# Expert rows added to token sums in DRAM by an accumulating indirect DMA

## What is computed

```python
out = jnp.zeros_like(t)
for e in range(N_EXPERTS):                       # 16
    hid = jax.nn.silu(t @ w_gate[e]) * (t @ w_up[e])
    out = out + combine[:, e:e + 1] * (hid @ w_down[e])
...
x = x + _hmoe(_rmsnorm(x, g_ffn), ...)
y = _rmsnorm(x, g_final)
```

## Time and profile before

| | us |
|---|---|
| median of 3 runs | 1064.77 |
| lowest, highest | 1064.41, 1065.37 |
| the profiled execution's own time | 1067.34 |
| its span, first to last instruction | 1065.6 |
| PE busy | 970.6 (91%) |
| DVE, ACT, POOL busy | 656.9, 547.8, 279.2 |

### The profile page before, as it was taken

The page is one execution under the profiler, slowest core; times in us unless marked ns, Lnnn a source line. Parts: engine busy times, 40 slices in busy tenths (PEclk is TensorE's granted clock), DMA queues, the critical chain, the costliest instruction groups (busy, mean ns, idle before and its releaser), DMA issues.

```text
span 1065.6 us, 16632 instructions
## 1 busy us (share of the span) xinstructions
PE 970.6 (91%) x5991; PEld 856.6 (80%) x5991; DVE 656.9 (62%) x797; ACT 547.8 (51%) x609; POOL 279.2 (26%) x187
## 2 busy tenths in 40 slices
PE   3989899999999998999999999939899999999960
PEld 2989789978988996799999986827788888888750
DVE  5495649647774884611211112378999898989827
ACT  5644525624462553533333323356787878787622
POOL 2433304213140331443434353000311010101012
PEclk9999999999999999999999999969999999999985
DMA  9452122312221320132332359228999999999835
GB/s 305 134 166 60 46 58 73 85 39 69 79 64 39 89 59 20 49 91 79 90 88 79 99 177 303 83 106 284 408 413 414 413 414 413 414 413 414 313 125 202
DMA packets 146738, 193.67 MB, mean 182 GB/s; under 512 B 14486, under 2 KB 91692, under 8 KB 146576
## 3 DMA queue, kind: packets, MB, share of 16 engines
q1 hardware_dynamic: 139000, 165.27, 44.9%
q0 software_dynamic: 4656, 16.21, 4.0%
q10 hardware_dynamic: 3048, 11.75, 2.8%
HBM read 173.43 MB, written 19.77 MB: 181 GB/s over the span
## 4 chain that ended last, share of the span: by engine, by line
PE 71%; DVE 14%; issue 7%; ACT 4%; DMA 2%; DVEq 1%; POOL 0%; POOLq 0%; ACTq 0%; SPq 0%
PE PJ L447 58%; DVE MEM L1640 2%; DVE MEM_R L1859 2%; PE NM L1272 2%; PE PJ L1221 1%; PE MS L1455 1%; PE MS L1254 1%; PE MS L1292 1%; PE NM L447 1%; PE MS L1267 1%; PE MS L1299 1%; PE NM L1403 1%; PE MS L1282 1%; DMA MEM<-in_x_prompt_dram 1%; DMA MEM<-expert_rows,MEM 1%
## 5 line engine op out<-in xcount | busy, mean ns | idle before, releaser
L447 PE MATMUL PJ<-MEM_R 128*128 128x272 f32 (+2 forms) x5016 | 805.1, 321 | 14.5 <-ACT MEM L857 6.0
L447 PEld LDWEIGHTS PJ<-MEM_R 128*128 128x128 f32 x5016 | 723.9, 191 | 77.8 <-issue 10.6
L661 POOL TENSOR_TENSOR MEM_R<-RAW,MEM_R 128x1024 fp32r<-128x1024 f32 x81 | 198.5, 2459 | 357.1 <-ACT MEM_R L798 357.1
L1859 DVE TENSOR_TENSOR MEM_R<-CHUNK,MEM_R 128x2048 fp32r<-128x2048 f32 x100 | 224.6, 2286 | 15.4 <-ACT MEM_R L1055 14.1
L1055 ACT CAST MEM_R<-CHUNK 128x2048 fp32r<-128x2048 f32 x100 | 189.3, 1912 | 14.1 <-PE PJ L447 7.8
L798 ACT CAST MEM_R<-RAW 128x1024 fp32r<-128x1024 f32 x81 | 84.5, 1051 | 125.3 <-DMA RAW<-in_w_pb_dram 35.6
L1799 DVE TENSOR_TENSOR MERGED<-PJ,MEM 128x544 f32<-128x544 f32 x16 | 11.6, 724 | 146.9 <-PE PJ L447 146.9
L747 POOL COPY MEM<-MEM 128x1 uint32 (+1 forms) x16 | 20.7, 1297 | 235.1 <-PE MS L1455 235.1
L1640 DVE SCALAR_TENSOR_TENSOR MEM<-MEM 128x548 f32<-128x548 f32 x72 | 60.9, 846 | 8.5 <-DVE MEM L1638 0.9
L1064 ACT CAST MEM_R<-MS 128x1024 fp32r<-128x1024 f32 x17 | 17.3, 1016 | 33.6 <-PE MS L1455 33.6
L862 ACT ACTIVATE MEM<-MEM 128x548 f32<-128x548 f32 x16 | 10.6, 664 | 43.9 <-DVE MEM L1640 43.7
(11 more groups left out here) (282 smaller groups left out, 916.9 us busy)
## 6 DMA issues: line engine op xcount, KB each, us to landing
CHUNK<-in_w_gate_dram SPq DMA_DIRECT2D x34, 1024.0 KB, 9.7
CHUNK<-in_w_up_dram SPq DMA_DIRECT2D x34, 1024.0 KB, 11.3
CHUNK<-in_w_down_dram SPq DMA_DIRECT2D x34, 1024.0 KB, 9.7
RAW<-in_w_in_dram SPq DMA_DIRECT2D x56, 512.0 KB, 3.7
expert_rows<-MEM ACTq DMA_DIRECT2D x16, 512.0 KB, 6.0
expert_rows<-MEM SPq DMA_DIRECT2D x8, 512.0 KB, 5.2
RAW<-in_w_pa_dram SPq DMA_DIRECT2D x8, 512.0 KB, 3.6
RAW<-in_w_pb_dram SPq DMA_DIRECT2D x8, 512.0 KB, 3.6
```

The costliest lines, as they stand in the source:

```text
L447: ins = pe.matmul(out, w(a), x(b), start=first and n == 0, stop=last and n == 2)
L661: tt(lo, raw[slot], hi.bitcast(F32), ALU.subtract).then_inc(lo_done, 1)
L1859: tt(moe_hl[c][1], moe_raw[c], moe_hl[c][0].bitcast(F32), ALU.subtract).then_inc(chunk_lo[c], 1)
```

## The change

Two DRAM tensors are new. `token_sums` has one row for each token; POOL stores the residual `x2` there before the second gather. `choice_weights` has one word for each pair of token and expert: DVE makes it (`choice`), POOL stores it. DVE also makes `choice_id`, which is 16 times the token plus the tile's expert, for each place.

Empty places now hold 544, one more than the last token. The gather, the gather of weights and the scatter have a bounds check that skips such places; the gather's tile is cleared once, so that skipped rows hold something.

After a tile's gather POOL waits until ACT has copied the result out, then adds it to `token_sums` with an accumulating indirect DMA, then gathers the next tile's 128 weights into one column. ACT multiplies by this column as it copies the result out. An accumulation is only started after the one before it has landed. The last tile waits in the same way, and then SP loads the sums in five plain loads; the ten gathers and DVE's `add_rows` are gone. So are `expert_rows`, its stores, and the zero tile. `choice_weights` stands before `stage(1)`, and two DVE instructions on slots are gone. POOL's wait for the second gather's tile and the two new stores stand before its `stage(1)`.

```diff
             for m in range(NE, TILES):
-                sp.dma_start(y_dram[m * P:(m + 1) * P, :], zeros).then_inc(rows_zeroed, 16)
...
+            await_step(sp, sums_out, last * 16 + 16 * (J + 1))
+            for j in range(J):
+                sp.dma_start(ya[0:rows_of[j], j, :], sums_dram[tok(j), :]).then_inc(ya_in[j], 16)
...
+            pool.memset(xg, 0.0).then_inc(xg_cleared, 1)
+            pool.wait_ge(xg_cleared, 1)
             def gather_rows(index):
-                pool.indirect_dma_start(out=xg, out_offset=None, in_=t_dram,
-                                        in_offset=bass.IndirectOffsetOnAxis(ap=index, axis=0)).then_inc(xg_in, 16)
+                pool.indirect_dma_start(out=xg, out_offset=None, in_=t_dram, in_offset=row(index),
+                                        bounds_check=N - 1, oob_is_err=False).then_inc(xg_in, 16)
+            def gather_weight(out, index, landed):
+                pool.indirect_dma_start(out=out, out_offset=None, in_=choice_dram, in_offset=row(index),
+                                        bounds_check=N * NE - 1, oob_is_err=False).then_inc(landed, 16)
+            def add_to_sums(index, rows):
+                pool.indirect_dma_start(out=sums_dram, out_offset=row(index), in_=rows, in_offset=None,
+                                        bounds_check=N - 1, oob_is_err=False, compute_op=ALU.add).then_inc(sums_out, 16)
+            def scatter(i):
+                await_step(pool, y_ready, i)
+                pool.tensor_copy(place_id, ids[:, ds(i - 1, 1)]).then_inc(place_copied, 1)
+                await_step(pool, place_copied, i)
+                add_to_sums(place_id, yt)
             gather_rows(ids[:, 0:1])
+            for j in range(J):
+                pool.dma_start(sums_dram[tok(j), :], x2[0:rows_of[j], j, :]).then_inc(sums_out, 16)
             pool.wait_ge(xT_full, 1)
             gather_rows(ids[:, 1:2])
+            pool.wait_ge(xT_full, 2)
+            gather(2)
+            pool.wait_ge(choice_ready, 1)
+            pool.dma_start(choice_dram[0:LP * NE, :].rearrange("(j p e) a -> p j (e a)", p=P, e=NE), choice[:, 0:JP, :]).then_inc(choice_out, 16)
+            pool.dma_start(choice_dram[LP * NE:N * NE, :].rearrange("(p e) a -> p (e a)", e=NE), choice[0:LS, JP, :]).then_inc(choice_out, 16)
+            pool.wait_ge(choice_out, 32)
+            gather_weight(row_w[:, 0:1], choice_id[:, 0:1], row_w_in)
+            pool.wait_ge(sums_out, 16 * J)
             def stage(i):
                 await_step(pool, xT_full, i + 2)
                 gather(i + 2)
-            stage(0)
+                scatter(i)
+                pool.tensor_copy(w_id, choice_id[:, ds(i, 1)]).then_inc(w_copied, 1)
+                await_step(pool, w_copied, i)
+                gather_weight(row_w[:, 0:1], w_id, row_w_in)
...
-            pool.wait_ge(moe_done, 1)
-            for j in range(J):
-                n = rows_of[j]
-                for m, dst in enumerate((ya, yb)):
-                    pool.indirect_dma_start(out=dst[0:n, j, :], out_offset=None, in_=y_dram,
...
+            scatter(last)
+            await_step(pool, last_copied, 2)
+            await_step(pool, sums_out, last * 16 + 16 * J)
...
+            add_to_sums(place_id, last_rows)
...
-                await_step(act, y_out, i * 16)
-                act.copy(yt, PJ[:, 2:4, :].rearrange("p a n -> p (a n)")).then_inc(y_ready, 1)
-                act.wait_ge(y_ready, i)
-                act.dma_start(y_dram[ds(i * P - P, P), :], yt).then_inc(y_out, 16)
+                await_step(act, sums_out, i * 16 + 16 * (J - 1))
+                await_step(act, row_w_in, i * 16)
+                act.activation(yt, PJ[:, 2:4, :].rearrange("p a n -> p (a n)"), ACT.Copy, scale=row_w[:, 0:1]).then_inc(y_ready, 1)
...
-                L(stt(a12, t12, float(P), r12, ALU.mult, ALU.add))
-                L(dve.tensor_copy(slot_i, a12))
...
-                st.do(tt(w2, w1, dv, ALU.mult))
+                L(tt(w2, w1, dv, ALU.mult))
+                for m, w in enumerate((w1, w2)):
+                    st.do(tt(tp12[:, m], A12[:, m], spread(w, NE), ALU.mult))
+                st.wait()
+                st.do(tt(choice, tp12[:, 0], tp12[:, 1], ALU.add))
+                L(stt(choice_id, ids, float(NE), te, ALU.mult, ALU.add))
+                dve.sem_inc(choice_ready, 1)
...
+            choice_weights()
             stage(1)
-            choice_weights()
```

More of the change, by code:

```diff
@@ L238, in hawk_mlstm_hmoe_kernel @@
         x2_junk = at("rs", D // 2)
-        zeros = at("my", D, plus=(KT - 2) * N)
         V1C = {"cw": 0, "cb": TAPS * NCT, "lam": TAPS * NCT + NCT}
@@ L322, in hawk_mlstm_hmoe_kernel @@
         is_extra = late(J * D, 2, J, NX)
-        slot_i = small(2, J).bitcast(U32)
+        choice = small(J, NE)
+        choice_id = small(TAB).bitcast(U32)
+        row_w = small(2)
         te_i = small(TAB).bitcast(I32)
@@ L333, in hawk_mlstm_hmoe_kernel @@
         yt = at("sig", D)
-        idcur = at("small", 2, plus=60).bitcast(U32)
+        row_id, place_id, w_id, last_w_id = (at("small", 1, plus=60 + m).bitcast(U32) for m in range(4))
         assert cuts["v1"] + D <= cuts["cols"] and cuts["sig"] + D <= cuts["counts"]
@@ L510, in _ @@
             load_state(0)
-            for m in range(NE, TILES):
-                sp.dma_start(y_dram[m * P:(m + 1) * P, :], zeros).then_inc(rows_zeroed, 16)
             sp.wait_ge(pj_full, PJ_A0)
@@ L704, in late_const, with count @@
                 ins.then_inc(late_consts, 1)
-            def count(out, pattern, mult=0):
-                late_const(pool.iota(out, pattern=pattern, base=0, channel_multiplier=mult, allow_small_or_imprecise_dtypes=True))
+            def count(out, pattern, mult=0, base=0):
+                late_const(pool.iota(out, pattern=pattern, base=base, channel_multiplier=mult, allow_small_or_imprecise_dtypes=True))
             pool.wait_ge(mix_full, 4 * NCT2)
@@ L720, in _ @@
             late_const(pool.memset(ssq, 0.0))
-            pool.wait_ge(late_consts, LATE_CONSTS[0])
-            for x in (tok_in, tok_first):
-                late_const(pool.affine_select(out=x, in_=x, compare_op=ALU.is_ge, fill=0.0, base=N - 1,
-                                              pattern=[[-P, J]], channel_multiplier=-1))
+            late_const(pool.memset(row_w, 0.0))
             for c in range(5, 8):
@@ L1131, in _ @@
                 act.wait_ge(last_full, half + 1)
-                act.copy(last_rows[:, cols], PJ[:, half, :]).then_inc(last_copied, 1)
-                act.wait_ge(last_copied, half + 1)
-                act.dma_start(y_dram[ds(last * P, P), cols], last_rows[:, cols]).then_inc(y_out, 16)
-            await_step(act, y_out, last * 16 + 48)
-            act.sem_inc(moe_done, 1)
+                act.activation(last_rows[:, cols], PJ[:, half, :], ACT.Copy, scale=row_w[:, 1:2]).then_inc(last_copied, 1)
             for group in FIN_SETS:
@@ L1139, in _ @@
                     n = rows_of[j]
-                    act.wait_ge(sum_ready, j + 1)
-                    act.activation(ya[0:n, j, :], fin[0:n, j, :], ACT.Square, accum_out=ssq[0:n, j:j + 1]).then_inc(sum_squares, 1)
+                    act.wait_ge(ya_in[j], 16)
+                    act.activation(yb[0:n, j, :], ya[0:n, j, :], ACT.Square, accum_out=ssq[0:n, j:j + 1]).then_inc(sum_squares, 1)
                 cols = slice(group[0], group[-1] + 1)
```

56 lines of the change are left out of this document (26 added, 30 removed).

## The result

The changed kernel takes 1075.44 us in the median (1074.26 to 1078.13, 4 runs), the kernel before 1064.59 beside it: the ratio is 1.0104, with a 95% interval of 1.0083 to 1.0125. Its time is 1% longer, where 1061.9 was forecast and 1069.5 was the upper end of the range. The profiled execution took 1076.32 us, with a span of 1074.5.

A forecast was written before the change was run, and what follows sets the result against it. The prediction took TensorE (PE) to bound the steady expert tiles, with DVE's chain at their start and a serial tail. Its terms -0.4 + 4.1 - 6.6 = -2.9 took 1064.77 to 1061.9 us, range 1056.5 to 1069.5.

The forecast's parts named there:

- first gather -0.4: First gather at the start: skipping empty places moves 0.26 MB less, a gain of 0.4 us.
- The new wait, X = 761, term +4.1: Second tile: ACT's copy waits for row weights landing at X = 761; PE's fourth tile 4.1 us late, 2.2 from waiting.
- the ten DVE instructions: Weights' arithmetic, six moved and four new instructions, ahead of stage 1 on DVE's chain to PE: 2.2 us.
- the granted clock fell in the stall: Sign of a wrong forecast: TensorE's granted clock, 1.00 before, falling in the third tile's stall.
- the prediction's estimate from a rule of the Trainium skill: Second tile: POOL's copies and gathers contend with DVE's subtractions, X two to three us later, forecast near 1064.4.
- The steady tiles, cost 0, gain 0: Steady expert tiles: POOL's added work fits and PE is the bound, so nothing is lost or won.
- The tail, -6.6: After the last product: two additions of 5.4 us and five plain loads replace ten gathers, ending 6.6 us earlier.
- rival 3: Slow additions, two in a row at the end at 9 us each: 1069.1; chance 0.26 together with rival 2.
- Rival 2: ACT's new wait for weights before result 1 eats the tail's gain: 1068.9 at X = 768; chance 0.26 with rival 3.
- Rival 4: Skipped places still move their bytes, losing the first gather's 0.4 us and some tail gain: 1062.5; chance 0.06.
- Wrong would be: a longer period: Sign of a wrong forecast: the 17.80 us between steady tiles growing longer.

The follow-up runs named there:

- e1: The changed kernel with each tile's filled places spread over all 128 partitions instead of the first ones: 1070.85 us.
- e4: The changed kernel without the additions of tiles 0 to 14; the last two and the weights' gather remain: 1061.61 us.
- e12: e6 with rows written plainly into a table of 2 x 544 rows, nothing added in DRAM; DVE adds x2 and both halves: 1065.53 us.
- e10: e6 without the addition in its indirect DMAs, so that sums are overwritten: 1053.20 us.
- e6: The changed kernel with both the early choice weights of e5 and the spread places of e1: 1066.48 us.
- e2: The changed kernel with a plain indirect scatter in place of the addition, so rows overwrite the token's row: 1060.56 us.
- e5: The changed kernel with the choice weights computed earlier, before DVE's first gate; additions stay: 1073.0 us.
- e8: The changed kernel with each addition replaced by a plain gather of the sum rows into scratch and a plain scatter: 1074.23 us.

## Why the prediction was wrong

- **Start, first gather -0.4**: it landed in 4.35 us, against 4.30, so there was no gain. It also started 1.4 us later after the NM products. Half a us is POOL's: 0.80 us pass there before the gather instead of 0.28, in all the kernels with the change. The rest is the router's last eight products, 1.91 us instead of 1.08: in the 5 us around them the granted clock read 0.50, and 0.83 before. e1 to e4 have 1.07 there, so this part is not the change's.
- **The new wait, X = 761, term +4.1**: right in size, and partly by luck. The copy started at 760.18, and measured from the NM products the stretch grew by 4.5 us before rounding (122.24 against 117.75). But of these, 1.4 are the late first gather, which was not forecast. 2.1 are the ten DVE instructions, which stand in the chain as forecast (2.2). Only 1.0 came behind the third tile's start, where the wait was to cost 2.2, and there the chain does not pass through the wait at all:

```profile
756.62 12.49 PE PJ L451 x48
769.12 0.87 PE MS L1484 x8
769.99 5.58 PE PJ L451 x24
775.57 0.44 PE NM L1515 x4
```

  PE went on to the fourth tile at 776.01 without waiting; DVE, which the wait had made late, had its operand ready at 774.83. The third tile's 48 products took 12.49 us instead of 11.17, because the granted clock fell in the stall, which the text had named as a sign of being wrong. Without that, both would have been ready at about 774.8, so the wait was close behind. The two to three us by which the prediction's estimate from a rule of the Trainium skill (SBUF — State Buffer, section "Who interferes with whom") would have moved X did not come. The windows of the changed kernel, columns as above:

```profile
750.00:755.00 5.00, 0.79 (x4) 0.31 (x2) 5.00 (x4) 1.90 (x1) 1.29 (x1) 0.77 1.01 349
755.00:760.00 5.00, 4.49 (x13) 3.46 (x14) 5.00 (x4) 0.00 (x0) 3.54 (x3) 0.55 0.98 366
760.00:765.00 5.00, 5.00 (x24) 4.14 (x23) 2.77 (x3) 4.82 (x4) 2.63 (x3) 1.00 1.01 339
```

- **The steady tiles, cost 0, gain 0**: this is the step that failed, by 14.0 us. It counted the bytes of the queue ("loses the 0.5 MB store and half of the gather and gains about 0.27 MB that is added") and took an added byte for a moved byte. An added row holds an engine 327 ns where a plainly written one holds it 159, so nothing was left of the saving: 38 engine-us a tile beside the weights, before and after. Where the filled places lie costs 4.2 us more (e1). The weights' packets also took 275 engine-us a tile instead of 254, half of the difference with the additions; the cause of that is open. And the step rested on "PE is the bound" without asking by how much. The margin could be had from the trace of before: 13.6 us for a chunk against landings of 9.6 to 12.2 in the loaded stretch, 1.4 to 4.0 us, and the engines already full. The argument on POOL and ACT was right: POOL's issues fitted, and ACT did not wait for weights or sums in each tile.
- **The tail, -6.6**: right in sign and nearly in size (-7.8). The additions took 6.23 and 4.46 us, where 5.4 each had been taken: the sum fits, and that is luck in part. Neither tile is half-empty, as the text had it. The one before the last has 119 filled places (queue 0 moved 0.49 MB for it), the last one 6 (0.03 MB). Behind the additions the tail was 1.3 us shorter than forecast. By the fit of the Trainium skill (DMA: Bandwidth & Descriptors, section "Anatomy of one DMA — SWDGE (gpsimd) path") the two would take, as estimates, 3.1 and 2.1 us. The trace agrees roughly for plain writes (3.36 in e12 and 4.25 in e10 for the 119 rows, 2.27 in e10 for the 6) and not for additions (6.23 and 4.46 after, 6.24 and 3.60 in e6).
- **The rivals**: rival 3 spoke of slow additions and had the right sentence in it, "beyond some 11 us in the loaded stretch ACT would also wait in each tile, 15 times, and the time would go past 1075". The time is 1075.4, but by another way: the additions landed in 10.9 us, and ACT waited not for them but for the chunks beside them. Rival 2's wait came, at the forecast moment, and did not decide. Rival 4 is refuted: queue 0 moved 13.51 MB, and the 1088 rows gathered, the 1088 added and the 1088 stored into `t_rows` and `token_sums` are 13.4 of them. Empty places would have added 8.9.
- **The range** ended at 1069.5 because no case in it had a longer period. "Wrong would be: a longer period" was the right alarm for a case that had been given no chance.

## What to carry to other kernels

Before an engine's stretch is costed at nothing "because another engine is the bound", work out the margin: here the round of one buffer (load, high part, low part) against PE's 17.80 us, which leaves a load 13.6 us. Watch the landing times of the loads, not the busy share of the DMA engines: that share read 1.00 to 1.04 with PE fully busy and with PE starved. An accumulating DMA should be counted as a read and a write of its rows, and half as many of them may cost nothing where all of them cost ten us. And count the time that packets hold the engines, tile by tile and with the loads' own packets in it: here those grew by 21 engine-us a tile while everything beside them stayed at 38.

## What the runs showed of the hardware

- An accumulating indirect DMA has the same packets and bytes on the page as a plain one (146050 and 180.10 MB in both) and holds the engines some 11 to 13 engine-us longer for 64 rows of 4 KB (327 ns a row against 159). A plain scatter of the same rows holds them 9 to 10: 64 rows of 159 ns are 10.2, and e2 has 577 engine-us on queue 0 against 458 in e4 (3.4% and 2.7% of the span's), some 9 for each of 15 scatters, when e4's two remaining additions are counted.
- Which partitions hold the filled rows of a half-empty indirect DMA matters: spread over the tile they gave 4.6 us in the change (1075.4 to 1070.9 in e1) and 6.5 with early weights (e5 to e6). The traces name no engine for a packet, so that the load on the single engines evens out is argued, not shown.
- TensorE's granted clock fell while PE waited for the third tile (busy for 0.79 of 5 us) and read 0.55, near its lower level of 1.2 GHz, over the next 5 us, though PE was busy for 4.49 of them; 1.00 (2.4 GHz) came only after 760 us.
- Still open: why the weights' packets hold the engines longer in the changed kernel than before, even with plain writes (265 against 254 engine-us a tile in e2). Whether the adding itself costs anything beside the second pass over the rows; e8 bounds it at little. And whether x2 and the sums could be finished in the end without DVE's serial adds was not tried.
